# Norm borders of a 13-phase fp32 block kernel: last tile in token halves, high parts first, one sum for the double norm

## What is computed

```python
def rmsnorm(x, g):
    xf = x.astype(jnp.float32)
    y = xf * lax.rsqrt(jnp.mean(xf * xf, axis=-1, keepdims=True) + EPS)
    return y * g.astype(jnp.float32)

def modulate(x, g, shift, scale):
    return (rmsnorm(x, g) * (1.0 + scale) + shift).astype(x.dtype)
...
        h = modulate(x, norm_ffn_g[layer], sh_f, sc_f)
        x = x + (g_f * conv_glu_ffn(h, ffn_w_in[layer], ffn_conv_w[layer], ffn_conv_b[layer],
                                    ffn_w_out[layer])).astype(x.dtype)
    return rmsnorm(x, final_g).astype(x.dtype)
```

## Time and profile before

| | |
|---|---|
| runs of the kernel | 1993.88, 1997.53, 2000.53 us; median 1997.53 |
| profiled execution, span from first to last instruction | 1991.7 us |
| busy: TensorE, VectorE, ScalarE, GpSimd | 97%, 52%, 23%, 60% |
| mean granted TensorE clock | 0.986 of 2.4 GHz |
| the chain that ended last | TensorE 89%, VectorE 4%, ScalarE 3% |
| the costliest lines | the gemm's three matmuls, L446 to L448, some 631 us each |

### The profile page before, as it was taken

How to read it: one execution, slowest core, us unless ns; L and a number is a source line. 1 busy time by engine, 2 the same in 40 slices (tenths; PEclk the granted TensorE clock), 3 DMA queues, 4 the chain that set the end, 5 groups by cost and what they waited for, 6 DMA issues and landing times.

```text
span 1991.7 us, 25332 instructions
## 1 busy us (share of the span) xinstructions
PE 1926.6 (97%) x8824; PEld 1554.2 (78%) x8824; DVE 1033.4 (52%) x1529; ACT 452.7 (23%) x774; POOL 1185.3 (60%) x907
## 2 busy tenths in 40 slices
PE   5999999999999999999999999999998899999998
PEld 4787868888888887667888888886776688888886
DVE  7566256666655453566766663334847453333222
ACT  3302342121110022342211121023118421111100
POOL 3743326788887956325687877743550256666773
PEclk7999999999999999999999999998999999999999
DMA  7532223555555422111455553322220023222332
GB/s 304 178 116 75 95 95 106 182 194 193 190 191 189 159 95 83 61 44 63 159 190 191 188 199 108 109 91 64 85 68 19 24 84 105 95 95 95 105 106 74
DMA packets 67375, 242.23 MB, mean 122 GB/s; under 512 B 7498, under 2 KB 7882, under 8 KB 67314
## 3 DMA queue, kind: packets, MB, share of 16 engines
q1 hardware_dynamic: 65536, 237.01, 34.4%
q10 hardware_dynamic: 1778, 4.37, 0.6%
HBM read 239.25 MB, written 2.10 MB: 121 GB/s over the span
## 4 chain that ended last, share of the span: by engine, by line
PE 89%; DVE 4%; ACT 3%; issue 2%; DMA 2%; POOL 1%; SPq 0%; ACTq 0%; DVEq 0%; POOLq 0%
PE gemm L446 24%; PE gemm L447 23%; PE gemm L448 23%; PE gemm L473 2%; PE gemm L475 2%; PE gemm L474 2%; DMA w_raw<-wstream 2%; PE mix L649 1%; PE gemm L802 1%; PE mix L446 1%; PE gemm L1036 1%; DVE sq_acc L1355 1%; PE mix L447 1%; PE mix L448 1%; PE gemm L816 1%
## 5 line engine op out<-in xcount | busy, mean ns | idle before, releaser
L430 POOL TENSOR_TENSOR w_lo<-w_raw,w_hi 128x1024 fp32r<-128x1024 f32 x302 | 735.7, 2436 | 25.2
L446 PE MATMUL gemm<-h_hi,w_hi 128*128 128x512 f32 x1616 | 634.4, 393 | 21.7 <-DVE h_lo L1176 14.9
L447 PE MATMUL gemm<-h_lo,w_hi 128*128 128x512 f32 x1616 | 631.0, 390 | 0.0
L448 PE MATMUL gemm<-h_hi,w_lo 128*128 128x512 f32 x1616 | 630.9, 390 | 0.0
L427 POOL TENSOR_TENSOR pool_gate<-pool_gate 128x1 f32<-128x1 f32 x298 | 118.3, 397 | 736.0 <-PE gemm L448 596.1
L446 PEld LDWEIGHTS gemm<-h_hi,w_hi 128*128 128x128 f32 x1616 | 304.7, 189 | 90.7 <-issue 22.6
L448 PEld LDWEIGHTS gemm<-h_hi,w_lo 128*128 128x128 f32 x1616 | 304.6, 188 | 63.8
L428 POOL TENSOR_SCALAR w_hi<-w_raw 128x1024 fp32r<-128x1024 f32 x302 | 344.2, 1140 | 16.9 <-DMA w_raw<-wstream 16.9
L447 PEld LDWEIGHTS gemm<-h_lo,w_hi 128*128 128x128 f32 x1616 | 304.7, 189 | 62.4
L1070 DVE CUSTOM_DVE_ANT_0 ada_raw<-ada_raw,c_act 128x1024 f32<-128x1024 f32 x128 | 218.3, 1722 | 108.4 <-DMA ada_raw<-adastream 108.4
L448 PE MATMUL gemm<-p_hi,w_lo 128*128 128x512 f32 x528 | 205.4, 389 | 0.0
(11 more groups left out here) (341 smaller groups left out, 1970.4 us busy)
## 6 DMA issues: line engine op xcount, KB each, us to landing
w_raw<-wstream SPq DMA_DIRECT2D x302, 512.0 KB, 3.5
ada_raw<-adastream SPq DMA_DIRECT2D x128, 512.0 KB, 4.3
a_early<-adastream SPq DMA_DIRECT2D x8, 1024.0 KB, 11.8
out<-x_res SPq DMA_DIRECT2D x8, 256.0 KB, 2.2
c_act<-c_in ACTq DMA_DIRECT2D x2, 512.0 KB, 7.2
x_res<-x_in SPq DMA_DIRECT2D x2, 512.0 KB, 6.2
x_res<-x_in ACTq DMA_DIRECT2D x2, 512.0 KB, 9.1
b_dist<-const_in ACTq DMA_DIRECT2D x1, 512.0 KB
```

The costliest lines, as they stand in the source:

```text
L430: pool.tensor_tensor(wlo[s][:], raw[:, u % RAW, :], whi[s][:].bitcast(F32), ALU.subtract).then_inc(w_split, 1)
L446: pe.matmul(out_ap, w_h, r_h, start=first, stop=False)
L447: pe.matmul(out_ap, w_h, r_l, start=False, stop=False)
L448: return pe.matmul(out_ap, w_l, r_h, start=False, stop=last)
```

## The change

- `first_tiles` waits for the high part of a k block, runs the two products with it for all its tiles, and runs the product with the low part one k block later.
- At a border the last residual, the last square, the two first column sums, the spread and the first scaled tile with its high part are done in halves of 256 tokens. The first two blocks of 128 tokens are spread into the bank `M[0]`, then all four into `rstdps`. `squares` is written out with fixed addresses.
- At r = 4 a single inverse is taken: the squares are of `x` times the root of `final_g`² + eps, so that one root with eps² as its bias gives the product of both inverses. The plain sum's last square, root and inverse come behind, since the first norm's result is needed later; it is spread after the first tiles.
- `WARM` is smaller.
- At r = 6 the first tile of the output is scaled in halves.

```diff
-WARM = (2, 4, 4, 14)
+WARM = (1, 1, 2, 14)
...
+                def low(k):
+
+                    pe.wait_ge(h_ready, KT * fill + k + 1)
+                    for u in range(count):
+                        s = (N0[phase] + u) % SPL
+                        mm = pe.matmul(G[u][:], whi[s][:, k * P:(k + 1) * P], Hlo[:, k, :], start=False, stop=(k == KT - 1))
+                        if k == KT - 1:
+                            mm.then_inc(pe_done, 1)
+
                 for u in range(count):
                     pe.wait_ge(gfree[u], G0[phase][u])
                 for k in range(KT):
                     if k in before:
                         before[k]()
-                    pe.wait_ge(h_ready, KT * fill + k + 1)
+                    w = slice(k * P, (k + 1) * P)
+                    pe.wait_ge(hhi_ready, KT * fill + k + 1)
                     for u in range(count):
                         if k == 0 and u % 2 == 0:
                             pe.wait_ge(w_split, N0[phase] + u + 2)
                         s = (N0[phase] + u) % SPL
-                        mm = three(G[u][:], whi[s][:, k * P:(k + 1) * P], wlo[s][:, k * P:(k + 1) * P],
-                                   Hhi[:, k, :], Hlo[:, k, :], k == 0, k == KT - 1)
-                        if k == KT - 1:
-                            mm.then_inc(pe_done, 1)
+                        pe.matmul(G[u][:], whi[s][:, w], Hhi[:, k, :], start=(k == 0), stop=False)
+                        pe.matmul(G[u][:], wlo[s][:, w], Hhi[:, k, :], start=False, stop=False)
+                    if k:
+                        low(k - 1)
+                low(KT - 1)
...
+            def partial_sums(c0, tile, first, last, blocks=range(NTB)):
+
+                for j in blocks:
...
             def norm_scale(r):
 
+                borders[0] += 1
                 pe.wait_ge(sq_added, KT * r + KT - 1)
                 partial_sums(0, sqacc, True, False)
-                keep_warm(WARM[0])
-                pe.wait_ge(sq_ready, KT * (r + 1))
-                mm = partial_sums(0, sqt[:, 1, :], False, True)
+                c0, last = 0, sqt[:, 1, :]
                 if r == 4:
                     pe.wait_ge(gsq_added, KT)
-                    partial_sums(4, work[:, 2, :], False, False)
+                    c0, last = 8, work[:, 1, :]
+                    partial_sums(c0, work[:, 2, :], False, False)
+                keep_warm(WARM[0])
+                pe.wait_ge(sq_half, borders[0])
+                partial_sums(c0, last, False, True, (0, 1))
+                if r == 4:
                     pe.wait_ge(gsq_ready, KT)
-                    mm = partial_sums(4, work[:, 1, :], False, True)
-                mm.then_inc(norm_sum, 1)
-                keep_warm(3 if r == 4 else 1)
-
...
+                    pe.wait_ge(sq_ready, KT * (r + 1))
+                partial_sums(c0, last, False, True, (2, 3)).then_inc(norm_sum, 1)
+                keep_warm(WARM[1])
...
             def norm(r):
                 norm_scale(r)
+                c0 = 8 if r == 4 else 0
                 bc[0] += 1
-                bcast(rstdps, bc[0])
-                if r not in (0, 6):
-                    keep_warm(WARM[2])
+                pe.wait_ge(rstd_ready, bc[0])
+                token_rows(M[0], c0, (0, 1)).then_inc(bc_half, 1)
+                token_rows(rstdps, c0, (2, 3, 0, 1)).then_inc(rstd_bc, 1)
+                if r == 4:
+                    pe.wait_ge(sq_ready, KT * (r + 1))
+                    partial_sums(0, sqt[:, 1, :], False, True).then_inc(norm_sum, 1)
+                elif r != 6:
+                    keep_warm(WARM[2], M[1])
...
-            norm_scale(4)
-            bc[0] += 1
-            bcast(rstdps, bc[0] + 1, 8)
-            keep_warm(WARM[2])
-
+            norm(4)
             first_tiles("idx_in", FILL["idx_in"])
...
+            def last_residual(n, m, bank, gate):
+
+                dve.wait_ge(pe_done, n + 1)
+                for half, done in ((slice(0, HALF), last_half), (slice(HALF, T), gfree[bank])):
+                    dve.scalar_tensor_tensor(out=X[:, m, half], in0=G[bank][:, half], scalar=modv[:, gate + m:gate + m + 1],
+                                             in1=X[:, m, half], op0=ALU.mult, op1=ALU.add).then_inc(done, 1)
...
+            def border_inverses(c0):
+
+                borders[0] += 1
+                rms_n[0] += 1
+                dve.wait_ge(rms_ready, rms_n[0])
+                ready(dve.reciprocal(rst[:, c0:c0 + 4], rms[:, c0:c0 + 4]))
+                dve.wait_ge(bc_half, borders[0])
...
-                if first_gain is None:
-                    ready(inverse_rms(4, rms_n[0]))
-                else:
-                    ready(inverse_rms(4, rms_n[0]))
-                    dve.wait_ge(rstd_ready, inverses_done[0])
-
-                    rms_n[0] += 1
+                if first_gain is not None:
                     link(dve.tensor_tensor(a, a, first_gain, ALU.mult))
-                    link(dve.tensor_tensor(rst[:, 4:8], rst[:, 0:4], rst[:, 0:4], ALU.mult))
-                    dve.tensor_tensor(rst[:, 4:8], rst[:, 4:8], normps[:, 4:8], ALU.mult).then_inc(sig("second_mean"), 1)
-                    dve.wait_ge(rms_ready, rms_n[0])
-                    link(dve.reciprocal(rst[:, 8:12], rms[:, 8:12]))
-                    ready(dve.tensor_tensor(rst[:, 8:12], rst[:, 8:12], rst[:, 0:4], ALU.mult))
-                spread()
...
+                border_inverses(0 if first_gain is None else 8)
+
+                def scaled(k, part=slice(0, T), done=t_ready, bank=rstdps):
+                    dve.scalar_tensor_tensor(out=work[:, k % 4, part], in0=X[:, k, part], scalar=a[:, k:k + 1], in1=bank[:, part],
+                                             op0=ALU.mult, op1=ALU.mult).then_inc(done, 1)
...
-                scaled(0)
+                scaled(0, slice(0, HALF), t_half, M[0])
+                spread()
+                scaled(0, slice(HALF, T))
                 scaled(1)
                 for k in range(KT):
                     low(k)
                     if k + 2 < KT:
                         scaled(k + 2)
+                if first_gain is not None:
+                    rms_n[0] += 1
+                    ready(inverse_rms(4, rms_n[0]))
...
                 if not done:
-                    rms_n[0] += 1
-                    ready(inverse_rms(4, rms_n[0]))
+                    border_inverses(0)
+                    dve.scalar_tensor_tensor(out=X[:, 0, 0:HALF], in0=X[:, 0, 0:HALF], scalar=g[:, 0:1], in1=M[0][:, 0:HALF],
+                                             op0=ALU.mult, op1=ALU.mult)
                 spread()
-                for k in range(KT):
+                if not done:
+                    dve.scalar_tensor_tensor(out=X[:, 0, HALF:T], in0=X[:, 0, HALF:T], scalar=g[:, 0:1], in1=bank[:, HALF:T],
+                                             op0=ALU.mult, op1=ALU.mult).then_inc(sig("x_normed"), 1)
+                for k in range(0 if done else 1, KT):
                     dve.scalar_tensor_tensor(out=X[:, k, :], in0=X[:, k, :], scalar=g[:, k:k + 1], in1=bank[:],
                                              op0=ALU.mult, op1=ALU.mult).then_inc(sig("x_normed"), 1)
...
+            def roots(c0, bias):
+
                 nrm[0] += 1
                 act.wait_ge(norm_sum, nrm[0])
-                act.activation(rms[:, 0:4], normps[:, 0:4], ACT.Sqrt, bias=col("eps"), scale=1.0 / D).then_inc(rms_ready, 1)
+                act.activation(rms[:, c0:c0 + 4], normps[:, c0:c0 + 4], ACT.Sqrt, bias=bias, scale=1.0 / D).then_inc(rms_ready, 1)
...
             def high_tiles(shift):
-                for k in range(KT):
+                act.wait_ge(t_half, borders[0])
+                act.activation(Hhi[:, 0, 0:HALF], work[:, 0, 0:HALF], ACT.Identity, bias=modv[:, shift:shift + 1])
+                act.wait_ge(t_ready, scaled[0] + 1)
+                act.activation(Hhi[:, 0, HALF:T], work[:, 0, HALF:T], ACT.Identity, bias=modv[:, shift:shift + 1]).then_inc(hhi_ready, 1)
+                for k in range(1, KT):
 
                     act.wait_ge(t_ready, scaled[0] + k + 1)
                     act.activation(Hhi[:, k, :], work[:, k % 4, :], ACT.Identity, bias=modv[:, shift + k:shift + k + 1]).then_inc(hhi_ready, 1)
...
             def squares(r, phase, gain=None):
 
                 act.preload_act_table(ACT.Sqrt)
-                with act.Fori(0, 2) as i:
-                    for u in range(4):
-
-                        act.wait_ge(gfree[u], i + G0[phase][u] + 1)
-                        act.wait_ge(sq_added, 4 * i + KT * r + u - 1)
-                        square(4 * i + u, u % 2)
-                        if gain is not None:
-                            act.wait_ge(gsq_added, 4 * i + u + 1)
-                            act.activation(work[:, u % 2, :], X[:, ds(4 * i + u, 1), :].rearrange("p a t -> p (a t)"), ACT.Square,
-                                           scale=cols[:, ds(4 * i + gain + u, 1)]).then_inc(gsq_ready, 1)
+                if gain is not None:
```

(37 more changed lines are left out.)

52 lines of the change are left out of this document (25 added, 27 removed).

## The result

The changed kernel takes 2030.3 us (median of 4, 2028.0 to 2032.0) where the kernel before takes 1997.5 us (median of 4, 1993.9 to 2000.5): a ratio of 1.0176 over the runs, 95% interval 1.0161 to 1.0192 (the two medians alone give 1.0164). Forecast were 1983.9 us and a gain of 13.6 us. The profiled execution has a span of 2026.1 us, 34.4 us above that of before.

A forecast was written before the change was run, and what follows sets the result against it. TensorE, busy 97% of 1991.7 us, was taken as the bound, so only its waits and filler could be won: 2.6 + 1.0 + 1.7 + 5.75 + 0.3 + 2.2 = 13.6 us off 1997.5, giving 1983.9 us; 8-in-10 range 1978.5 to 1990.0.

The forecast's parts named there:

- Does the lead survive?: First tiles after a border: low parts ready at 350.2, wanted at 350.8 with passes of 0.227 us; TensorE carries the lead on.
- the 0.04 for something I don't see: Chance of 0.04 left for something unseen that eats all of the gain.
- the first fill: First fill, high first: gemm starts at 28.9 us and goes on at 62.4 after the fill; gain 2.2 us, bounds nothing to 3.5.
- the border at 950: Border at 952 us: squares start sooner, the 0.4 us wait for running squares is won; gain 1.7 us, between 0.4 and 1.7.
- Borders at 334 and 1613: Two borders between gemm phases: halves and high-first order bring the first gemm 1.3 us earlier at each, 2.6 us together.
- Border at 701: Border at 701 us: loads issued from ScalarE's queue delay the root by 0.3 us; gain 1.0 us, 1.3 if issues slip forward.
- Double norm: Border at 1318 us with two norms, now one chain: first gemm at 1325.4 instead of 1331.15, gain 5.75 us.
- The rival with 0.22: The clock falls again in the double norm, 2.6 us back: 1986.5 us; chance 0.22.
- Last border: Border at 1979 us, ending in the output: earlier spread and half a scaled tile gain 0.3 us.
- The rival of halves that don't overlap: Paired halves run strictly one after the other, costing 0.8 us per border over five borders: 1987.9 us; chance 0.08.
- The rival of the clock at every border: Lost warm-ups let the clock fall at every border, 4.6 us each at four, 2.6 at the double norm: 2004.9 us; chance 0.04.
- my sign of being wrong: Wrong if the clock drops below 1.00 in any border; one of three signs named, no size given.

The follow-up runs named there:

- the two runs that differ in placement alone: The changed kernel as it is (2030.3 us), and the same with one existing 32-byte tensor allocated ahead of the weights instead of behind them (1986.4 us).
- the repaired kernel: The changed kernel with its epsilon column in the GpSimd gate's tensor, all other tensors at the addresses of before: 1987.0 us, ratio 0.9959 to the kernel before.
- 18 and 5 fillers: Changed kernel at the old addresses plus 18 fillers behind the first fill and 5 ahead of the running-square sums at 950 us: 1990.7 us, ratio 0.9976.
- the kernel before with 64 bytes: The kernel before with 64 unused bytes per partition where the change allocates its epsilon column, moving every tensor behind: 2010.4 us, ratio 1.0085.
- moved `rms`: The kernel before with its 128-byte tensor `rms` allocated ahead of the weights instead of behind them: 2035.3 us, ratio 1.0196.
- 64 bytes too: The changed kernel with 32 more bytes behind its epsilon column, so everything behind stands 64 bytes above its place before: 2004.7 us, ratio 1.0058.
- 6 and 2 fillers: Changed kernel with 6 fillers behind the first fill and 2 ahead of the running-square sums at 950 us: 1982.9 us, ratio 0.9937 to the kernel before.

## Why the prediction was wrong

**The step that failed** is none of the sum's terms but the assumption under them, that the gemm passes keep their pitch. "Does the lead survive?" counts with 0.227 us a pass after the change as before it. The passes went to 0.2333, by that 47 us in all (44 between the two runs that differ in placement alone), because of the one line of the diff that I had taken for bookkeeping. No rival had it; the 0.04 for something I don't see was the only place for it, and the slow side had too little. Nothing in the profile of before could show it, but the diff could: it moves one of two operand tensors in memory.

**Two terms of the sum failed too**, the first fill and the border at 950, and with the two losses under "Not in the sum" they are why the change on the old distances gains half of the 13.6 us. Neither has a price for new idle and what the clock does behind it. The terms, in the repaired kernel:

- **Borders at 334 and 1613** (1.3 each): 1.41 and 1.41. Right. In the rows of the border at 337 us the residual pair took 0.88 (my ends at 334.63 and 335.50 give 0.87), the sums started 1.12 us after the residual (1.09), the spread took 1.60 (1.66). The lead did survive the first tiles: 1,584 passes behind it took 358.93 us, before 358.90.
- **Border at 701** (1.0): 1.20, between my 1.0 and 1.3.
- **Border at 950** (1.7, at least 0.4): -0.75. The sum of squares on VectorE, not TensorE, sets when this border can begin. Each addition took as much longer as its square came sooner, so coming earlier only lengthened TensorE's wait; and I gave no price to the clock here. In the other changed kernels without fillers the gap is 8.03, 8.74, 10.31 and 10.34 us (before: 7.97), as the clock falls for a shorter or longer time: -0.1 to -2.4. With two fillers and the clock at 1.00 it is 7.61, still only 0.4 better than before.
- **Double norm** (5.75): 5.97. Right, and the clock held: the first gemm came 7.05 us after the last pass, at 1.00 throughout. The rival with 0.22 came true in one of the seven changed kernels alone, the one with 18 and 5 fillers, and cost 1.3 us where I said 2.6.
- **Last border** (0.3): 6.05 of lead at the last gemm, 6.44 in the span: 0.4. Right.
- **First fill** (2.2, at least nothing): first gemm at 28.6 and gemm after the fill at 62.1, as forecast (28.9, 62.4), and then nothing of it left. The mechanism was right as far as 62 us; what I did not follow is that TensorE would now idle 3.1 us and take up the gemm at half clock.
- **Not in the sum:** the gap at 187 us was 6.31 before and 8.00 in the repaired kernel. The wait in it is the same 2.6 us, but the clock falls behind it (0.50 from 190.8 us). It takes one of these two values in kernels of either kind: 8.00 also in the kernel before with 64 bytes and with moved `rms`, and in the three other changed kernels at distance 0 without fillers or with too many; 6.31 or 6.32 in the other placements of the kernel before, in the changed kernel itself, with 64 bytes too, and with 6 and 2 fillers. I can't lay it to a step of the change. The same goes for a loss of 1.4 us in the index stage: from the end of the double norm to the end of its second gap it takes 57.2 us before and 58.6 in the repaired kernel, and from 55.9 to 58.6 over all kernels at distance 0.

**The rival of halves that don't overlap** falls: the halves of the residual take 0.88 us as a pair where the whole takes 0.75, and the border is still 1.4 us shorter. The Trainium skill, VectorE: DVE Perf Modes, "The TRN2 errata", has each instruction pay a fixed cost, and the trace agrees: 0.13 us for the split.

**The rival of the clock at every border** (0.04) was right in kind and too dear. No changed kernel had a fall in every border, but each of the seven had one in at least one of the five ahead of the last: four in the border at 950 alone (the changed kernel of the result among them), one there and in the border at 334, one in the double norm, and the one with 6 and 2 fillers at 1613. A fall made the border 0.4 to 2.7 us longer than the shortest like it, where I said 4.6. So my sign of being wrong, a clock below 1.00 in any border, came true in the changed kernel itself, at 970 us. The Trainium skill, TensorE: Matmul & The Clock Gate, "The HAM clock gate", calls the throttled state the default that activity lifts; the trace agrees with it at 62 us, where 2.8 us of filler was enough to keep 1.00.

## What to carry to other kernels

When passes that the change didn't touch all become longer by the same few ns, compare the addresses of their operands before any wait or order: an innocent allocation ahead of the working buffers moves them. Keep the moving and the stationary tensor of 512-column rounded passes a multiple of 256 bytes apart, new small tensors behind the large ones or in unused columns of old ones; in each A/B comparison hold the layout fixed, or half the experiments measure it. And time won ahead of a fixed wait becomes idle, which in the first fill cost nearly all of it again in half clock; a counted number of filler passes kept it, and too many cost more than they saved.

## What the runs showed of the hardware that I had not expected

- A 128x512 pass of rounded float32 takes 0.2267 us or up to 0.2343 us, a difference of 3%, by the distance of its two operands in SBUF modulo 256 bytes: 0 is best, 64 costs 0.0022, all other multiples of 32 cost 0.0057 to 0.0076 (table above). Absolute addresses don't count (ratio 0.9998 and 1.0006 with all moved), nor do copies on VectorE and GpSimd beside the passes.
- Unrounded float32 passes lose nothing at the distances tried (0.8583 us a pass of 512 columns, 0.2233 of 128), nor do rounded passes of 256 columns (0.1200 at distance 0, 0.1184 and 0.1200 at two others). Why the distance counts is not settled.
- The clock fell to 1.2 GHz behind a wait of 3.1 us (at 62 us); in some kernels and not in others behind the same wait of 2.6 us at 187 us; and in the border at 950 behind a wait of 1.3 us followed by narrow and filler passes.
